# Attention scores and chunk states on whole 128x128 TensorE tiles in place of 64x64 quadrants

## The reference

```python
b = jnp.cumsum(gk, axis=3)
q_d = q * jnp.exp(b)
k_d = k * jnp.exp(-b)
scores = jnp.einsum('bhnid,bhnjd->bhnij', q_d, k_d)
scores = jnp.where(tril, scores, 0.0)
o_intra = jnp.einsum('bhnij,bhnje->bhnie', scores, v)
k_end = k * jnp.exp(b_last - b)
chunk_state = jnp.einsum('bhncd,bhnce->bhnde', k_end, v)
def step(S, inp):
    dec, cs = inp
    return dec[..., None] * S + cs, S
...
o_inter = jnp.einsum('bhncd,bhnde->bhnce', q_d, S_prev)
o = o_intra + o_inter
```

## Time and profile before

| | before |
|---|---|
| median of 3 runs | 1571.57 us (1571.01 to 1571.81) |
| the profiled execution, own time | 1571.57 us |
| its span in the trace | 1570.1 us |
| PE busy | 1442.4 us, 92% of the span |
| DVE, ACT, POOL busy | 48%, 37%, 21% |
| mean granted TensorE clock | 0.972 of full speed |

### The profile page before, as it was taken

The page is one execution under the profiler, slowest core; times in us unless marked ns, Lnnn a source line. Parts: engine busy times, 40 slices in busy tenths (PEclk is TensorE's granted clock), DMA queues, the critical chain, the costliest instruction groups (busy, mean ns, idle before and its releaser), DMA issues.

```text
span 1570.1 us, 28228 instructions
## 1 busy us (share of the span) xinstructions
PE 1442.4 (92%) x11714; PEld 1042.9 (66%) x11714; DVE 746.9 (48%) x1221; ACT 577.3 (37%) x973; POOL 334.9 (21%) x298
## 2 busy tenths in 40 slices
PE   3259699999999999999999999999999999999985
PEld 2238576766768676776867576676867676676752
DVE  2775626455361726445262635436172645526162
ACT  1344424344342424334242434434242433424231
POOL 1321303031220303122221303122030313122110
PEclk9679799999999999999999999999999999999998
DMA  8130100101020010102010010102001010201001
GB/s 339 56 134 2 41 1 28 54 13 67 0 80 0 27 53 27 53 0 80 0 63 17 27 53 18 62 0 80 0 27 53 27 53 0 80 0 54 1 28 67
DMA packets 15432, 69.32 MB, mean 44 GB/s; under 512 B 2352, under 2 KB 2480, under 8 KB 12848
## 3 DMA queue, kind: packets, MB, share of 16 engines
q1 hardware_dynamic: 15408, 68.98, 11.9%
HBM read 52.20 MB, written 16.78 MB: 44 GB/s over the span
## 4 chain that ended last, share of the span: by engine, by line
PE 82%; DVE 8%; ACT 3%; issue 3%; POOL 2%; DMA 1%; SPq 1%; ACTq 0%; POOLq 0%; DVEq 0%
PE bank L330 69%; PE bank L467 2%; PE bank L475 2%; PE bank L481 2%; PE bank L489 2%; PE bank L532 1%; DVE whl L836 1%; DVE arena L979 1%; DVE nm L988 1%; DVE arena L997 1%; POOL arena L1156 1%; ACT arena L715 1%; PE bank L383 1%; DVE arena L962 1%; DVE mx L985 1%
## 5 line engine op out<-in xcount | busy, mean ns | idle before, releaser
L330 PE MATMUL bank<-arena,whl 128*128 128x256 f16 x6144 | 683.8, 274 | 3.0 <-DVE whl L836 3.0
L330 PEld LDWEIGHTS bank<-arena,whl 128*128 128x128 f16 x6144 | 601.6, 98 | 84.5 <-issue 7.0
L330 PE MATMUL bank<-arena 128*128 128x512 f16 x1536 | 343.5, 381 | 12.3 <-DVE arena L856 12.3
L330 PEld LDWEIGHTS bank<-arena 128*128 128x128 f16 x1536 | 148.2, 98 | 184.8 <-issue 18.6
L947 DVE SCALAR_TENSOR_TENSOR arena<-arena 64x256 f32<-64x256 f32 x60 | 25.2, 420 | 411.9 <-POOL arena L1173 410.5
L330 PE MATMUL bank<-whl,arena 128*128 128x512 f16 x768 | 168.4, 379 | 0.0
L676 ACT ACTIVATE arena<-bank,sca 128x512 f32<-128x512 f32 x64 | 43.9, 687 | 262.8 <-PE bank L330 261.7
L330 PEld LDWEIGHTS bank<-whl,arena 128*128 128x128 f16 x768 | 75.1, 98 | 87.3
L1156 POOL TENSOR_TENSOR arena<-arena 128x512 f16<-128x512 f32 x64 | 89.5, 1410 | 142.3 <-ACT arena L724 142.3
L1166 POOL TENSOR_TENSOR arena<-arena 128x542 f32<-128x542 f32 x16 | 17.3, 1079 | 463.9 <-issue 438.8
L867 DVE SCALAR_TENSOR_TENSOR arena<-bank,sca,arena 128x512 f32<-128x512 f32 x64 | 47.8, 749 | 108.0 <-PE bank L330 91.4
(11 more groups left out here) (154 smaller groups left out, 1516.0 us busy)
## 6 DMA issues: line engine op xcount, KB each, us to landing
arena<-in_xt SPq DMA_DIRECT2D x16, 1024.0 KB, 5.4
arena<-in_x SPq DMA_DIRECT2D x32, 512.0 KB, 3.4
out<-arena SPq DMA_DIRECT2D x32, 512.0 KB, 2.6
arena<-in_w_in SPq DMA_DIRECT2D x8, 768.0 KB, 16.1
arena<-in_w_out SPq DMA_DIRECT2D x1, 4096.0 KB, 12.2
arena<-in_w_in SPq DMA_DIRECT2D x8, 392.0 KB, 16.2
arena<-in_w_mem SPq DMA_DIRECT2D x1, 2048.0 KB, 10.9
arena<-in_memt SPq DMA_DIRECT2D x1, 1024.0 KB, 6.5
```

Source lines behind the costliest of these rows:

```text
L330: mm = nc.tensor.matmul(ap, lhs, rhs, start=k == 0 and n == 0, stop=(k, n) == last)
```

## The change

The scores become one matmul for each pair of heads and each 128-token tile: 128 rows, 128 columns of weights and 256 moving columns (2 heads by 128 queries), 4 matmuls for 16. Tile t goes to bank 6 + t and has its own signal. Products between the two heads fall on the zeros of `qb`; products between the two chunks of a tile are computed and then not copied, since `causal` is zero there. The mask copy is one instruction for each tile over 128 partitions and 512 columns (2 for 4 of 64 partitions and 256 columns).

For the states the transposed keys go to a new layout `kab`, [NT * HEADS, 2, 64], in which the keys of an even chunk stand in rows 0 to 63 and columns 0 to 63, those of an odd chunk in rows 64 to 127 and columns 64 to 127, and the rest is zero. One matmul for each head and tile (128 rows, 128 weight columns, 128 moving columns) gives the states of both chunks: 8 matmuls for 16. The copy out of bank 4 becomes two ScalarE instructions of 64 partitions, and they now stand behind the squares of the next step. `state(c)` becomes 4 VectorE instructions of 64 partitions in place of 2 of 128. On TensorE `quarter(0)` no longer stands behind the wait for `ket_out`; some waits of the score part stand later. GpSimd clears `kab` once, in the first step.

```diff
-        ket = view(O_KAB, [NT, HEADS, DK], F32)
+        kab = view(O_KAB, [NT * HEADS, 2, 64], F32)
...
                 pe.wait_ge(ke_ok, i + 1)
-                pe.wait_ge(kd_ok, i + 1)
-                pe.wait_ge(q_ok, 2 * (i + 1))
                 if not first:
-                    pe.wait_ge(pt_out, 4 * i)
                     pe.wait_ge(mix_g, 2 * i)
...
                 mm.then_inc(pe_ket, 1)
+                pe.wait_ge(kd_ok, i + 1)
+                pe.wait_ge(q_ok, 2 * (i + 1))
                 for t in range(NT):
+                    if not first:
+                        pe.wait_ge(pt_out, 4 * i - 1 + t)
                     for p in range(NPAIR):
-                        n = t * NPAIR + p
-                        for odd in range(2):
-                            for h in range(2):
-                                r = slice(64 * h, 64 * h + 64)
-                                c = slice((2 * t + odd) * CHUNK, (2 * t + odd + 1) * CHUNK)
-                                mm = nc.tensor.matmul(bank[6 + h][64 * odd:64 * odd + 64, n * CHUNK:(n + 1) * CHUNK],
-                                                      kd[r, p, c], qb[r, p, h, c], start=True, stop=True,
-                                                      skip_group_check=True)
-                mm.then_inc(pe_sc, 1)
+                        mm = nc.tensor.matmul(bank[6 + t][:, p * 256:(p + 1) * 256], kd[:, p, t * P:(t + 1) * P],
+                                              qb[:, p, :, t * P:(t + 1) * P], start=True, stop=True)
+                    mm.then_inc(pe_sc, 1)
...
-                def states(t):
-                    for p in range(NPAIR):
-                        for odd in range(2):
-                            for e in range(2):
...
+                def states(t, b):
+                    for h in range(HEADS):
+                        mm = nc.tensor.matmul(bank[b][:, h * DV:(h + 1) * DV], kab[:, t * HEADS + h, :, :],
+                                              v[:, t, h * DV:(h + 1) * DV], start=True, stop=True)
+                    mm.then_inc(pe_st, 1)
...
-                pe.wait_ge(ket_out, i + 1)
+                quarter(0)
+                pe.wait_ge(ket_out, 2 * (i + 1))
                 pe.wait_ge(v_out, 2 * (i + 1))
-                quarter(0)
-                states(0)
-                states(1).then_inc(pe_st, 1)
+                states(0, 5)
+                states(1, 4)
...
-                nc.scalar.activation(ket, bank[4][:, :].rearrange("p (a b c) -> p a b c", a=NT, c=DK),
-                                     ACT.Copy).then_inc(ket_out, 1)
                 if not last:
...
                     squares(i + 1)
+                act.wait_ge(pe_ket, i + 1)
+                if first:
+                    act.wait_ge(cleared, 3)
+                for odd in range(2):
+                    r = slice(64 * odd, 64 * odd + 64)
+                    nc.scalar.activation(kab[r, :, odd, :], bank[4][r, :].rearrange("p (a b) -> p a b", b=64),
+                                         ACT.Copy).then_inc(ket_out, 1)
...
-                def masked(h):
+                mask = causal[:, :].bitcast(I32).unsqueeze(1).broadcast_to([P, 4, P])
+                def masked(t):
...
-                    for odd in range(2):
-                        r = slice(CHUNK * odd, CHUNK * odd + CHUNK)
-                        a = nc.vector.copy_predicated(s_head[r, :, h, r], mask[odd],
-                                                      bank[6 + h][r, 0:256].rearrange("p (a b) -> p a b", b=CHUNK))
-                    a.then_inc(sT_ok, 1)
+                    dve.wait_ge(pe_sc, 2 * i + t + 1)
+                    nc.vector.memset(idle[:, t:t + 1], 0.0)
+                    nc.vector.copy_predicated(sT[:, t, :, :], mask, bank[6 + t][:, :].rearrange("p (a b) -> p a b", b=P)
+                                              ).then_inc(sT_ok, 1)
...
-                    for p in range(NPAIR):
-                        n = t * NPAIR + p
+                    for h in range(HEADS):
+                        p, r = h // 2, slice(64 * (h % 2), 64 * (h % 2) + 64)
                         a = nc.vector.scalar_tensor_tensor(
-                            S[:, c + 1, p, :], S[:, c, p, :], dec[:, p, c:c + 1],
-                            bank[5 - odd][:, n * DV:(n + 1) * DV], ALU.mult, ALU.add)
+                            S[r, c + 1, p, :], S[r, c, p, :], dec[r, p, c:c + 1],
+                            bank[5 - t][64 * odd:64 * odd + 64, h * DV:(h + 1) * DV], ALU.mult, ALU.add)
...
+            nc.gpsimd.memset(kab, 0.0).then_inc(cleared, 1)
             nc.gpsimd.memset(sT, 0.0).then_inc(cleared, 1)
```

More of the change, by code:

```diff
@@ L445, in mem_scores @@
                     mm.then_inc(pe_ms, 1)
-                def states(t):
-                    for p in range(NPAIR):
-                        for odd in range(2):
-                            for e in range(2):
-                                rows, h = slice(64 * odd, 64 * odd + 64), 2 * p + e
-                                n = t * NPAIR + p
[L454 to L457, removed]
+                def states(t, b):
[3 more added lines that the diff above has]
+                    mm.then_inc(pe_st, 1)
                 def turn_p(n, b):
@@ L694, in step @@
                                          scale=2.0 ** -QBITS).then_inc(qm_hi, 1)
-                act.wait_ge(pe_ket, i + 1)
-                if first:
-                    act.wait_ge(lo_o, KT)
-                nc.scalar.activation(ket, bank[4][:, :].rearrange("p (a b c) -> p a b c", a=NT, c=DK),
-                                     ACT.Copy).then_inc(ket_out, 1)
                 if not last:
@@ L964, in step @@
                                                    ALU.subtract).then_inc(qm_lo, 1)
-                mask = [causal[r, r].bitcast(I32).unsqueeze(1).broadcast_to([CHUNK, 4, CHUNK])
-                        for r in (slice(0, CHUNK), slice(CHUNK, P))]
-                s_head = sT.rearrange("p t (a h) s -> p (t a) h s", h=2)
-                def masked(h):
+                mask = causal[:, :].bitcast(I32).unsqueeze(1).broadcast_to([P, 4, P])
+                def masked(t):
                     if first:
                         dve.wait_ge(built, 3)
-                        dve.wait_ge(cleared, 3)
-                    dve.wait_ge(pe_sc, i + 1)
-                    nc.vector.memset(idle[:, h:h + 1], 0.0)
-                    for odd in range(2):
-                        r = slice(CHUNK * odd, CHUNK * odd + CHUNK)
-                        a = nc.vector.copy_predicated(s_head[r, :, h, r], mask[odd],
-                                                      bank[6 + h][r, 0:256].rearrange("p (a b) -> p a b", b=CHUNK))
-                    a.then_inc(sT_ok, 1)
+                        dve.wait_ge(cleared, 4)
+                    dve.wait_ge(pe_sc, 2 * i + t + 1)
+                    nc.vector.memset(idle[:, t:t + 1], 0.0)
+                    nc.vector.copy_predicated(sT[:, t, :, :], mask, bank[6 + t][:, :].rearrange("p (a b) -> p a b", b=P)
+                                              ).then_inc(sT_ok, 1)
                 def mem_max(n):
@@ L1001, in state @@
                     t, odd = c // 2, c % 2
-                    dve.wait_ge(pe_st, i + 1)
+                    dve.wait_ge(pe_st, 2 * i + t + 1)
                     if c == 0:
```

## The result

The changed kernel takes 1590.78 us (median of 4 runs, 1589.22 to 1591.35) against 1571.69 us before (4 runs, 1571.01 to 1572.11): a ratio of 1.012, 95% interval 1.0103 to 1.0138. It is slower, as forecast, but by 19.1 us where 7.1 were forecast, and outside the range. The profiled execution has 1591.03 us, its span 1589.6 us.

A forecast was written before the change was run, and what follows sets the result against it. TensorE, busy 92% of the span, was taken to bound the kernel. Loop 14 x 0.41 = 5.7, first step 0.5 and last step 0.8 made 7.1 us on 1571.6: 1578.7 us, range 1574.0 to 1582.5.

The forecast's parts named there:

- Scores: TensorE before `mem_scores(0)`: 8 records take 1.74 us; 1.2 us more work fills the hole and costs nothing.
- States on TensorE: TensorE ahead of `mem_scores(2)`: 1.84 us for the old 1.03, so `turn_p(0)` starts 0.24 us later.
- First pair's chain: Softmax chain to `p_lo(0)`: earlier squares and folds bring it 0.49 us forward; mask copies' 0.4 us saving goes nowhere.
- Second pair's chain: Softmax chain to `turn_p(2)`, expected to bind: `mem_max(2)` 0.53 us later, a loop step +0.41 us.
- four more are +1.02 us: VectorE ahead of `mem_max(2)`: `state(0)` and `state(1)` become eight instructions, the four extra costing 0.255 us each.
- Rival 3: VectorE's eight narrow state instructions do not overlap, 0.34 us each; a step +0.89 us, total 1585.9 us; chance 0.10.
- Rival 4: Before `turn_p(0)`: states under about 1.3 us let the chain's 0.49 us come back each step, 1564.7 us; chance 0.04.
- First and last step: First step +0.53 us, VectorE setting the pace; last step +0.8 us, the states' whole extra time counting.
- Rival 2, the clock: First step: longer states in TensorE's idle stretch keep the clock up, 3 us come back, 1575.7 us; chance 0.15.

The follow-up runs named there:

- e6: The kernel before with ScalarE's squares ahead of the key copy, plus the full-tile scores and mask copies, old states kept; 1563.97 us, ratio 0.9950.
- e9: The kernel before with squares first, parts of three output quarters moved ahead, and full-tile scores and mask copies; 1558.57 us, ratio 0.9919.
- e1: The changed kernel with state(c) again 2 VectorE instructions of 128 partitions, half the rows using the wrong head's operand; 1572.85 us, ratio to before 1.0005.
- e5: The kernel before with ScalarE's squares ahead of the key copy and the wait for that copy moved into quarter(0); 1564.08 us, ratio 0.9951.
- e3: The kernel before with state(c) as 4 instructions of 64 partitions, heads 0, 1, 2, 3, source and target partitions equal; 1598.72 us, ratio 1.0174.

## Why the prediction was wrong in size

- *Scores*: right. 8 records issued in 1.73 us, 0.216 from start to start (1.74 forecast). `mem_scores(0)` did not move: it comes 2.46 us behind the key transposes in both kernels, and 2.02 instead of 1.93 behind the scores only because these start 0.09 earlier. The longer scores are shown free by e6, and shown dear without the hole by e9.
- *States on TensorE*: 1.78 us for a forecast of 1.84; `turn_p(0)` moved by 0.09 and not 0.24, since the states also start 0.10 us earlier (6.05 for 6.15 behind `mem_scores(0)`). The whole of TensorE's part is 0.10 us a step (e1).
- *First pair's chain*: right. The folds hold line 988 and the squares' place moves it by 0.49 (e5); the mask copies' saving is lost there (e6). They saved 0.69 and not 0.4: the two new copies overlap (0.75 each, 0.65 from start to start), and the two old ones of a pair, on different halves of the partitions, did not (0.44 each, 0.45 from start to start).
- *Second pair's chain*: the mechanism and the place were right, and this is the step that failed in size. The term "four more are +1.02 us" took 0.255 us for each instruction. Measured: 1.77. With 2.99 for 2.24 the chain is 1.28 late and not 0.53, and the same working gives 0.53 + 0.75 - 0.12 = 1.16 us a step, which is what the step grew by. The reason given, that 64 partitions take no less time than 128, is true of one instruction (0.33 to 0.36 us against 0.33 to 0.35). What was overlooked is that neighbours which alternate between the halves lose their overlap. It stood in the earlier trace rows: two mask copies on alternating halves take 0.90 us, which I halved as a duration and did not compare with the 0.255 of the wide pair.
- *Rival 3* named this cost, 0.34 each, and a time of 1585.9. It was given 0.10, and the range took in a quarter of it. It was still short: it left out the 0.10 us by which `state(1)` waits beyond that, and the price of a start behind a switch is a little over one duration, so the eight take 2.99 us and not 2.72. Its reason, that source and target partitions differ, was wrong (e3).
- *Rival 4* was misjudged in its condition. The 0.49 us come back in full only if the states take no more than 787.11 - 0.87 - 785.13 = 1.11 us, not 1.3, and in part up to 1.60. With the old states at 1.03 they do come back: that is e5, 1564.1 us.
- *First and last step*: +1.1 and +1.2 for 0.5 and 0.8. Of the last step's, 0.7 are there with wide state instructions too (e1). And 0.9 us ahead of the first attention part that no step of the prediction had. Over the other profiled kernels this stretch varies from 151.9 to 153.8 us without any change there, so I put no cause to it.
- *Rival 2, the clock*: in the changed kernel it did not come. The windows of the first step, in the kernel before (the one that the earlier trace rows does not show),

```profile
170.00:180.00 10.00, 10.00 (x70) 8.32 (x69) 5.03 (x5) 3.68 (x6) 0.37 (x1) 0.75 0.01 2
```

in the changed kernel,

```profile
160.00:170.00 10.00, 3.40 (x26) 2.16 (x24) 9.45 (x23) 5.92 (x18) 3.96 (x5) 0.66 0.00 0
170.00:180.00 10.00, 8.96 (x70) 8.51 (x72) 7.53 (x13) 2.72 (x5) 2.01 (x2) 0.65 0.00 0
```

and in e1:

```profile
160.00:170.00 10.00, 4.07 (x34) 3.05 (x35) 8.62 (x22) 5.22 (x15) 4.67 (x4) 0.70 0.00 0
170.00:180.00 10.00, 7.75 (x67) 6.12 (x64) 5.12 (x5) 6.04 (x10) 2.93 (x2) 0.96 0.00 0
```

The granted clock is 0.66 and 0.65 where it was 0.56 and 0.75: the stretch at 1.2 GHz has moved, not shrunk. In e1, with the same work on TensorE and the wide state instructions, it is 0.70 and 0.96, and the first step is 2.3 us shorter than before, where the earlier folds alone were worth 0.5 by the prediction. So the rival did come there. But its reason, the longer states in the idle stretch, is not needed: e5 has the old states and a first step of 84.75 us, 2.1 shorter. Both have the softmax chain earlier; that this is what keeps the clock up is not shown.

## What to carry to other kernels

Before replacing small matmuls by fewer large ones, read how long the group of small ones lasts in the timeline: quadrants that run together can be cheaper than full tiles, and padding is free only inside a hole that needed work could also fill. When a layout change splits another engine's instructions, price the split by the distance between starts of neighbours with the same pattern of partitions, not by one instruction's duration; order them so that the partitions change as seldom as possible. A hole in front of the bounding engine is the thing to fill first: with 1.3 us of output projection there, and parts of two more quarters moved with it, a step became 1.29 us shorter, more than anything in the change was worth.

## What the runs showed of the hardware

- Sixteen f32 matmuls of 64x64 by 128 columns in the four quadrants take 1.03 us, eight full ones 1.78; sixteen of 64 columns take 0.63, four full ones of 256 columns 1.73.
- Neighbouring VectorE instructions of 128 columns, with no wait between them, start 0.255 to 0.273 us apart on the same partitions and 0.341 to 0.370 apart when the start changes between 0 and 64.
- A VectorE instruction on two columns lasted 1.31, 0.82 or 1.55 us, each time ending within 0.03 us of the GpSimd instruction that had started before it, and 0.23 us with none beside it.
